# A two-block transformer forward pass on one core: another order of blocks in the second block's mixing stage

## What is computed

```python
h = _rms_norm(x, norm_mix_pre[l])
(a_q, a_k, a_v, f_q, f_k, f_v, f_g, c_u, s_x, s_b, s_c) = jnp.split(h @ w_in[l], cuts, axis=-1)
...
ya = _diff_attention(...)                 # branch 0
yf = _forgetting_attention(...)           # branch 1, log_f from f_g
c_a, c_g = jnp.split(c_u + b_glu[l], 2, axis=-1)
yc = _dwconv_causal(c_a * jax.nn.sigmoid(c_g), conv_dw[l]) + conv_dw_b[l]   # 31 taps, 512 channels
yc = jax.nn.silu(_layer_norm(yc, conv_ln_g[l], conv_ln_b[l]))               # branch 2
ys = s_b * _dwconv_causal(s_c * s_x, sc_w[l])                               # branch 3, 3 taps
br = jnp.stack([ya, yf, yc, ys], axis=2)
proj = jnp.einsum('bsnc,ncd->bsnd', br, w_branch[l])
gates = jax.nn.sigmoid(h @ w_gate[l] + b_gate[l]).reshape(B, S, N_BRANCH, D)
mixed = jnp.sum(gates * proj, axis=2) @ w_out[l]
```

## Time and profile before

| | us |
|---|---|
| median of three executions | 1425.2 |
| the profiled execution's own time | 1422.91 |
| its span, first to last instruction | 1421.0 |
| PE busy | 1304.8 (92%) |
| DVE busy | 842.1 (59%) |
| ACT busy | 664.0 (47%) |
| POOL busy | 125.9 (9%) |
| mean granted clock of TensorE | 0.962 of full speed |

### The profile page before, as it was taken

The page is one execution under the profiler, slowest core; times in us unless marked ns, Lnnn a source line. Parts: engine busy times, 40 slices in busy tenths (PEclk is TensorE's granted clock), DMA queues, the critical chain, the costliest instruction groups (busy, mean ns, idle before and its releaser), DMA issues.

```text
span 1421.0 us, 22163 instructions
## 1 busy us (share of the span) xinstructions
PE 1304.8 (92%) x9128; PEld 1218.4 (86%) x9128; DVE 842.1 (59%) x1081; ACT 664.0 (47%) x906; POOL 125.9 (9%) x172
## 2 busy tenths in 40 slices
PE   6997888999999998899999898689899987899997
PEld 5996878899998997799998898677899976799996
DVE  4864353765555654655556359986445573676664
ACT  4654445554445453444445343534444444554552
POOL 4420000100000001000000006350000000000000
PEclk9989999999999999999999899799899989899999
DMA  7740010556554543455554453422356533365551
GB/s 241 201 149 30 31 60 30 162 196 188 193 189 167 194 150 117 163 180 190 192 190 160 153 179 103 135 89 93 120 174 182 190 132 108 115 201 185 178 192 44
DMA packets 160465, 211.32 MB, mean 149 GB/s; under 512 B 5541, under 2 KB 143219, under 8 KB 160387
## 3 DMA queue, kind: packets, MB, share of 16 engines
q1 hardware_dynamic: 157299, 202.77, 44.1%
q0 software_dynamic: 2048, 7.37, 1.5%
q10 hardware_dynamic: 1040, 0.07, 0.0%
HBM read 209.14 MB, written 1.05 MB: 148 GB/s over the span
## 4 chain that ended last, share of the span: by engine, by line
PE 78%; DVE 12%; ACT 5%; issue 2%; DMA 1%; POOL 1%; DVEq 0%; SPq 0%; POOLq 0%; ACTq 0%
PE bank L305 23%; PE bank L308 23%; PE bank L309 23%; PE bank L1128 4%; DVE common L1983 3%; DVE wlo L299 2%; PE bank L1463 1%; ACT whi L291 1%; PE bank L1549 1%; ACT common L542 1%; DMA raw<-in_w_in 1%; DVE mx L1486 1%; PE bank L998 1%; DMA raw<-in_dn_w_in 1%; ACT common L1499 1%
## 5 line engine op out<-in xcount | busy, mean ns | idle before, releaser
L299 DVE TENSOR_TENSOR wlo<-raw,whi 128x2048 fp32r<-128x2048 f32 x191 | 437.5, 2292 | 270.3 <-ACT whi L291 270.3
L305 PE MATMUL bank<-xhi,whi 128*128 128x256 f32 x1824 | 525.8, 288 | 10.8 <-DVE xlo L610 9.4
L308 PE MATMUL bank<-xlo,whi 128*128 128x256 f32 x1824 | 522.3, 286 | 0.0
L309 PE MATMUL bank<-xhi,wlo 128*128 128x256 f32 x1824 | 522.2, 286 | 0.0
L291 ACT ACTIVATE whi<-raw 128x2048 fp32r<-128x2048 f32 x191 | 364.6, 1910 | 197.2 <-PE bank L305 137.1
L305 PEld LDWEIGHTS bank<-xhi,whi 128*128 128x128 f32 x1824 | 356.7, 196 | 15.2 <-issue 13.5
L308 PEld LDWEIGHTS bank<-xlo,whi 128*128 128x128 f32 x1824 | 356.4, 195 | 1.7
L309 PEld LDWEIGHTS bank<-xhi,wlo 128*128 128x128 f32 x1824 | 356.0, 195 | 0.0
L305 PE MATMUL bank<-whi,hhi 128*128 128x512 f32 x392 | 154.1, 393 | 2.7 <-DVE hlo L2450 2.5
L308 PE MATMUL bank<-wlo,hhi 128*128 128x512 f32 x392 | 153.6, 392 | 0.0
L309 PE MATMUL bank<-whi,hlo 128*128 128x512 f32 x392 | 153.1, 391 | 0.0
(11 more groups left out here) (310 smaller groups left out, 1585.6 us busy)
## 6 DMA issues: line engine op xcount, KB each, us to landing
raw<-in_mlp_w_up SPq DMA_DIRECT2D x32, 1024.0 KB, 5.4
raw<-in_mlp_w_down SPq DMA_DIRECT2D x32, 1024.0 KB, 4.8
raw<-in_w_in SPq DMA_DIRECT2D x22, 1024.0 KB, 5.0
raw<-in_w_up SPq DMA_DIRECT2D x22, 1024.0 KB, 5.0
raw<-in_dn_w_in SPq DMA_DIRECT2D x16, 1024.0 KB, 6.0
raw<-in_w_gate SPq DMA_DIRECT2D x16, 1024.0 KB, 5.7
raw<-in_mb_w_in SPq DMA_DIRECT2D x12, 1024.0 KB, 5.1
raw<-in_w_down SPq DMA_DIRECT2D x11, 1024.0 KB, 4.8
```

The source lines that it names most:

```text
L299: nc.vector.tensor_tensor(wlo[:, s, :], raw[:, V % RAW, :], f32(whi[:, s, :]), ALU.subtract).then_inc(lo_ready, 1)
L305: ins = pe.matmul(o, shi, mhi, start=first, stop=False, skip_group_check=True)
L308: pe.matmul(o, shi, mlo, start=False, stop=False, skip_group_check=True)
L309: return pe.matmul(o, slo, mhi, start=False, stop=last, skip_group_check=True)
```

## The change

The blocks of the stage stand in another order. The long convolution is first (e 0 to 3), then the short one (4 to 9), then the attention's 12 blocks as before. DVE's taps are spread over blocks 4 to 26 instead of 10 to 21, POOL does its 31 taps in one run before the two roots, and the short convolution's arithmetic (L1904 to L1912 of before) moves from the place after its own blocks into block 10. The narrow product of the forget gates follows block 0, which now starts as soon as the first half of the normalised input is there. The layer norm starts at block 28 (`LN`) instead of 22. In `MIX` all blocks (j, 0) with their gates come first (22 to 33), then all (j, 1) (34 to 47), with one `macc` for each j.

```diff
-            SHORT, CONV, TRIO, MIX = 0, 6, 10, 22
+            CONV, SHORT, TRIO, MIX = 0, 4, 10, 22
+            LN = MIX + 6
...
-            quota = [16, 16, 3] + 3 * [7, 12, 3]
+            quota = [6, 6, 6, 6, 5, 5] + [0, 3, 5] + [1, 3, 6] + [1, 3, 6] + [1, 4, 6] + [2, 4, 5, 4, 5]
...
+            order = [(0, 0), (0, 1), (1, 0), (1, 1), 0, (2, 0), (2, 1), 1, (3, 0), 2, (3, 1), 3]
+            for item in order:
+                if len(S) in (LN + 1, LN + 3, LN + 4):
+                    ln.append(bank().use())
...
-                        block_product(pe, b)
-                    if e == SHORT:
+                        block_product(pe, b, norm=None if e else norm)
+                    if e == CONV:
+                        gates0.pe(pe)
+                    elif e == CONV + 1:
                         gates0.pe_turn(pe)
...
-                    if e == MIX:
+                    if e == LN:
                         pe_mean(pe)
-                    elif e == MIX + 2:
+                    elif e == LN + 2:
                         pe_var(pe)
-                    elif e == MIX + 3:
+                    elif e == LN + 3:
                         pe_spread(pe)
...
-                    if e == CONV:
+                    if e == TRIO:
                         dve_short_conv(dve)
-                    elif e == CONV + 1:
+                    elif e == TRIO + 2:
                         dve_short_lo(dve)
...
-                    if TRIO <= e < MIX:
-                        dve_taps(dve, e - TRIO)
+                    if SHORT <= e < LN - 1:
+                        dve_taps(dve, e - SHORT)
...
-                pool_taps(pool, 0, 12)
+                pool_taps(pool, 0, 31)
                 heads[0].root(pool)
-                pool_taps(pool, 12, 20)
                 heads[1].root(pool)
-                pool_taps(pool, 20, 31)
                 pool_root(pool)
```

More of the change, by code:

```diff
@@ L1869, in bank @@
                 return G[(turn[0] - 1) % 2]
[L1871 removed]
+            CONV, SHORT, TRIO, MIX = 0, 4, 10, 22
+            LN = MIX + 6
             S = []
[L1875 to L1877 removed]
             pads = p2d.next()
+            sgc = common[:, 0:1024]
+            for j in range(4):
+                S.append(block_of(W, C0 + 256 * j, bank()))
+            sx, sbb = common[:, 1536:2560], common[:, 6776:7800]
+            su = common[:, 2560:2560 + 4 * 258].rearrange("p (f t) -> p f t", f=4)
+            sy = sx.rearrange("p (f t) -> p f t", f=4)
             for j in range(4):
@@ L1963, in block2 @@
             taps = [(j, f) for j in range(31) for f in range(DVE_TILES)]
-            quota = [16, 16, 3] + 3 * [7, 12, 3]
+            quota = [6, 6, 6, 6, 5, 5] + [0, 3, 5] + [1, 3, 6] + [1, 3, 6] + [1, 4, 6] + [2, 4, 5, 4, 5]
             quota = [sum(quota[:n]) for n in range(len(quota) + 1)]
-            assert len(quota) == MIX - TRIO + 1 and quota[-1] >= len(taps)
+            assert len(quota) == LN - SHORT and quota[-1] == len(taps)
             y_conv = Signal(sem("conv_summed")).next()
@@ L2027, in block2 @@
             added = Signal(sem("branch_added"))
[L2028 to L2031, removed]
+            prods, hi_m, lo_m = [added.many(1) for j in range(4)], [], []
+            sg = [[common[:, 0:512], common[:, 512:1024]], [common[:, 1024:1536], common[:, 6776:7288]]]
+            macc = [common[:, 7288:7800]] + [common[:, 1024 + 512 * j:1536 + 512 * j] for j in range(1, 4)]
+            heads, acc, gate_uses, ln = [], [], {}, []
             gate_at, branch_at, rows_at = {}, {}, {}
[L2033 to L2038, removed]
-                    S.append(block_of(WG, D * g + 256 * j, bank()))
[L2040 to L2047, removed]
+            order = [(0, 0), (0, 1), (1, 0), (1, 1), 0, (2, 0), (2, 1), 1, (3, 0), 2, (3, 1), 3]
+            for item in order:
+                if len(S) in (LN + 1, LN + 3, LN + 4):
+                    ln.append(bank().use())
+                if isinstance(item, tuple):
+                    j, g = item
+                    gate_at[len(S)] = item
+                    S.append(block_of(WG, D * g + 256 * j, bank()))
+                    gate_uses[item] = S[-1].use
+                    continue
+                if item == 0:
                     for n in range(4):
@@ L2063, in block2 @@
                             (lambda part, p_, m=m: (bhi, blo)[part][:, 4 + 2 * m + p_, :])))
-                for b in range(2):
-                    branch_at[len(S)] = (j, b)
-                    S.append(Block(U=unit(features(WB, 256 * j, row=D * b)), uses=[G[2 + b].use(), bank().use()]))
+                branch_at[len(S)] = (item, 0)
+                S.append(Block(U=unit(features(WB, 256 * item)), uses=[G[2].use(), bank().use()]))
+            for j in range(4):
+                prods[j] += added.many(2)
+                for g in (2, 3):
+                    gate_at[len(S)] = (j, g)
+                    S.append(block_of(WG, D * g + 256 * j, bank()))
+                    gate_uses[j, g] = S[-1].use
+                if j in (1, 2):
+                    if j == 1:
+                        acc.extend(b.use() for b in O)
+                    rows_at[len(S)] = j - 1
+                    S.append(Block(U=unit(rows(WO, 256 * (j - 1)))))
+                branch_at[len(S)] = (j, 1)
+                S.append(Block(U=unit(features(WB, 256 * j, row=D)), uses=[G[3].use(), bank().use()]))
                 hi_m.append(hid_sq.next())
@@ L2824, in _ @@
             norm_mix.pe_tile(pe, 1)
-            gates.pe(pe)
             mix.pe(pe)
```

67 lines of the change are left out of this document (32 added, 35 removed).

## The result

| | before | after |
|---|---|---|
| median of 4 executions, us | 1425.66 (1424.47 to 1426.25) | 1411.38 (1409.67 to 1412.71) |
| the profiled execution's own time, us | 1422.91 | 1412.05 |
| its span, us | 1421.0 | 1410.0 |
| mean granted clock of TensorE | 0.962 | 0.969 |

The ratio is 0.9900, with a 95% interval of 0.9883 to 0.9917: the kernel is faster by 14.3 us (11.8 to 16.7). The forecast was 1413.1 and the range 1398 to 1424.

What follows compares the result with a forecast made beforehand. PE, busy 92% of the span, was taken as the bound, so only its waits and the slow clock after them could be won: −6.5 −6.1 −1.4 −9.6 +11.5 = −12.1, from 1425.2 to 1413.1 us; range 1398 to 1424.

Steps and rivals of the forecast that it cites:

- to PE's turn of group 0: Stage start until PE turns group 0's probabilities: reached at 892.5 instead of 899.0, gain 6.5 us.
- gate −1.4: Between blocks 22 and 23: PE's wait for a gate's read-out goes, gain 1.4 us.
- layer norm −9.6 + 11.5: Layer norm, six blocks later: old waits and slow clock go, 9.6 us; new waits 8.0 and clock 3.5 cost 11.5.
- The head: Stage start: block 0 no longer waits for the narrow weights; gated input written at 813.9, 42 us earlier.
- DVE's way to group 0: Gated input to group 0's maximum: DVE's own low parts, taps and short convolution sum up to 881.7.
- The two waits ahead of it: Blocks 10 and 11: PE waits 3.2 and 1.3 us for banks DVE frees, hidden under group 0's wait of 13.
- Groups 1 and 2: Attention groups 1 and 2: cheaper taps cut PE's waits by 2.5 and 2.0 us; with slow clock, gain 6.1.
- the slow clock behind them: After the waits at groups 1 and 2: slow-clock losses of 1.0 and 0.6 us removed.
- Less hindrance: Rival, DVE's way to group 0: DVE and POOL hinder each other less; 1393 in full, 1403 at half; 20%.
- Full exclusion: Rival, DVE's taps beside POOL: the two exclude each other, 1.11 us a pair; 1424.1, no change; 6%.
- The clock: Rival, layer norm: blocks 30 to 35 all run slow, 2.8 us lost each; 1426, at half 1420; 8%.
- POOL's root: Rival, group 0's output: the root, behind all 31 POOL taps, comes after 903.4 and delays DVE; 1430; 8%.

Runs made afterwards that it cites:

- Experiment 1: The kernel after with the forget gates' narrow product again first, before block 0; 1417.38 us, ratio 0.9958.
- experiment 4: The kernel after with POOL's taps again in three stretches (12, 8, 11) around the roots; 1400.78 us, ratio 0.9855.
- experiment 6: The kernel before with only its 93 DVE taps dealt more evenly over the same twelve blocks; 1415.73 us, ratio 0.9928.
- 8: The kernel after with layer norm one block earlier, POOL's taps in three stretches, and 12 DVE taps moved behind group 0; 1383.74 us, ratio 0.9715.
- Experiment 3: The kernel after with the layer norm starting one block earlier, at 27 instead of 28; 1403.15 us, ratio 0.9848.
- experiment 2: The kernel after with POOL doing 3 of its 31 taps, so one convolution tile is incomplete; 1392.4 us, ratio 0.9782.
- version 10: As version 9, with the forget gates' narrow product behind block 1 and its turn behind block 2; 1388.04 us, ratio 0.9745.
- version 9: The kernel after with layer norm one block earlier, 12 DVE taps moved later, and POOL's taps in two stretches (12, 19); 1385.23 us, ratio 0.9728.
- experiment 7: The kernel after with layer norm one block earlier and POOL's taps in three stretches; 1387.64 us, ratio 0.9743.

## Why the prediction was right

The sum was −12.1 in the stage. The lengths of its parts in the two traces give, by the same steps:

| step | forecast | measured |
|---|---|---|
| to PE's turn of group 0 (head and DVE's way) | −6.5 | −4.6 |
| from there to the block behind group 2's turn | −6.1 | −9.1 |
| the rest of the stage: gate −1.4, layer norm −9.6 + 11.5 | +0.5 | +2.2 |
| sum | −12.1 | −11.5 |

Each part has the sign that was forecast, but the sum is as near as it is by luck: two errors of about 2 us and one of 3 the other way cancel.

**The head** came as worked out: the gated input was written at 813.0, relative, for 813.9. Experiment 1 shows its share: without it 6.0 of the 14.3 us are gone.

**DVE's way to group 0** was mis-sized by 2.7 us: 70.5 from the gated input to the maximum, not 67.8. The low parts were taken at 2.2 each. Beside POOL they take 2.7 to 2.8 from the second on, about 4 us more for the nine; the trace of before already had one beside POOL's taps, at 870.82, that took 2.70. The last five taps were all at 0.44, since POOL was done at 881.0, which is 878.2 relative, for the 882 forecast: 1.5 less. The short convolution, for which no row stood, took 10.95 for the 10.5 chosen. Its lower bound of 5.8 is what it takes with POOL idle (experiment 4, 5.7). The wait at group 0 was 12.5 for 13. The two waits ahead of it were 3.2 and 1.3 in the forecast; 3.5 was there, the second not, and in its place 1.9 for ACT's copy (L1422), all under the same cover.

**Groups 1 and 2.** Group 1's wait came out at 2.1 for 2.9, group 2's went. The mis-sized term is the slow clock behind them, 1.0 and 0.6 in the forecast. Group 1's turn took 0.87 instead of 1.54 and its block 6.00 instead of 7.96 (0.122 a matmul for 0.163); group 2's turn 1.47 for 2.65 and its block 5.99 for 6.58: 2.6 and 1.8. The turns' own matmuls had been left out, and group 1's block alone lost 2.0. Against it, the block behind group 0 was 0.5 slower. 3.3 + 2.0 + 2.6 + 1.8 − 0.5 is the 9.1, but for rounding. No experiment takes this part by itself. That it hangs on the taps and on POOL is read from others: in experiment 6, with 6 taps in place of 7 and POOL beside them, group 1 still waits 4.9, and with the new dealing and POOL beside it 3.6 and 3.8 (experiments 4 and 8), where it is 2.1 without.

**The layer norm.** Waits 2.9, 1.9, 1.9 and 0.5, for 3.1, 1.9, 2.2 and 0.8; slow clock 3.9 in the blocks (30, 31 and 32 at 0.151, 0.165 and 0.124) for 3.5, but 1.0 more in the variance's matmuls, which I had not counted, and a new half microsecond at the stage's last rows (0.8 for L2306, 0.3 before): 12.6 for 11.5. The old place gave 4.7 + 0.4 of waits and 4.3 of clock, 9.4 for 9.6, and the gate its 1.4 (the 2.8 of clock in the forecast set 50 matmuls against the time of 48; the block behind the 4.7 ran at 0.176 a matmul, 2.7 lost); 0.4 of the row's 2.2 stays in pieces too small to name. Experiment 3 takes the new waits away and gains 8.2, 11.8 by the stage: the change had given back here all that moving the layer norm won.

**The rivals.** *Less hindrance* is out: taps beside POOL took 0.82, and experiment 2 shows what it would have been worth, 19 us. *Full exclusion* of whole instructions is out too. The Trainium skill, page "SBUF — State Buffer", section "Who interferes with whom", has the second instruction block fully; here a tap and an instruction of POOL, 0.43 and at least 0.60 when alone, took 0.82 together, less than the 1.03 of one after the other. Whether a part of each excludes the other no run tells. A low part alone takes 2.29 and beside POOL 2.83, and one POOL instruction beside it takes 2.66: that one does wait for nearly all of it. *The clock* at half the full price is out, since only blocks 30 and 31 were slow: the sign set for it, a clock under 0.8, did show in these two (0.79 and 0.71), but blocks 32 to 35 ran at 0.118 to 0.124 a matmul. *POOL's root* had 27.2 us to spare.

The timed gain is 14.3 and that of the stage 11.5. The difference is inside what the start and the rest vary by, and it is not settled whether any of it belongs to the change.

## What to carry to other kernels

Work of GpSimd that shares the time of a busy VectorE is paid for on VectorE, here 0.35 to 0.39 us an instruction, where VectorE's instructions read only SBUF; those that read a PSUM bank, and the reductions, did not pay. So place it where VectorE is not what others wait for, or beside such instructions; one long run ahead of the first deadline cost 10.6 us against three stretches here. When a chain over several engines is hung into a regular sequence of blocks, look at what its links stand behind: one block earlier removed three waits and the slow clock behind them, 8 to 12 us. And before an order is rewritten, try the numbers in the old one: one line gave 8.8 of the 14.3 us.

## What was not expected of the hardware

- VectorE's low part (128 x 2048, two inputs) goes from 2.29 to 2.83 us when GpSimd works beside it, while GpSimd's own instruction, 0.60 to 0.74 when alone, takes 2.66: the long instruction loses 0.5, the short one waits for it. Of two short ones both lose (a pair of 0.43 and 0.60 takes 0.82). `tensor_scalar` with one tensor input, in SBUF, loses as well: L1524 from 1.01 to 1.77, the four of L1910 from 1.14 (experiment 4) to 2.95.
- Not every instruction of VectorE pays. In the kernel before, beside POOL's second stretch:

```profile
910.88 1.13 DVE L1645 TENSOR_SCALAR head_rows<-bank,mx 128x128 f32<-128x128 f32 x4 [1.21 <-POOL mx L1639]
911.92 1.94 DVE L1479 SCALAR_TENSOR_TENSOR common<-masks,bank 128x384 f32<-128x384 f32 x4
913.78 2.17 DVE L1486 TENSOR_REDUCE mx<-common 128x1 f32<-128x128 f32 x8
...
912.20 0.62 POOL L1996 TENSOR_TENSOR pool_product<-common,fc 128x256 f32<-128x256 f32 x1
912.90 0.74 POOL L2001 TENSOR_TENSOR common<-pool_product,common 128x256 f32<-128x256 f32 x1
```

  With POOL idle, at group 0, L1479 takes the same 1.94 and L1486 2.16, and L1645 takes 1.13 in experiment 2; POOL's instructions keep their 0.62 and 0.74. The first two read a PSUM bank, the third is a reduction. The short product L1897, which reads a bank too, takes 0.68 beside POOL and 0.69 without it (experiment 2).
- TensorE was granted 0.50 of full speed from 945 to 955 us in version 10, with no wait that version 9, at 1.00 there, did not have.
- Behind the same wait the clock differs: block 30, behind 2.9 us of waiting, ran at 0.151 a matmul after and at 0.121 in experiment 1. From the same waits, then, one block came out 1.4 us apart; a forecast of the slow clock behind one short wait is no better than that here.
- Kernels with the same program ahead of the stage reached it between 778.8 and 784.2. A difference of 3 us between two spans says little; the length of the stage added up where the medians did not (experiment 7).
